# Turning the raw input rows and applying the norm's root to the products: one edit to a hybrid mixer and MoE layer

## What is computed

```
h = rmsnorm(x, norm1_g)                 # x * rsqrt(mean(x*x) + eps) * g
u = h @ w_in                            # 2048 x 5632: a (3x512), q, k, v (1024 each), c (2x512)
y_a = bg * conv3(cg * xv)               # short convolution mixer
y_b = attention(q, k, v)                # 8 heads of 128, causal, with ALiBi
y_c = silu(layernorm(conv31(a * sigmoid(gate)) + b))
x = x + concat(y_a, y_b, y_c) @ w_out
x = x + moe(rmsnorm(x, norm2_g))        # 4 groups x 8 experts, top 2 within a group
out = rmsnorm(x, final_g)
```

## Time and profile before

| | |
|---|---|
| median of three runs | 1317.46 us |
| the profiled execution: span from first to last instruction | 1315.5 us |
| time around that span (median minus span) | 2.0 us |
| instructions | 15712 |
| TensorE products busy | 1236.0 us (94%) |
| VectorE, ScalarE, GpSimd busy | 557.6, 287.5, 6.0 us |
| HBM read and written | 469.13 and 2.10 MB |

### The profile page before, as it was taken

One profiled execution on the slowest core, in us unless ns is written; L12 is line 12 of the kernel. 1 busy time (PEld: TensorE's weight loads), 2 busy tenths in 40 slices (PEclk: granted clock), 3 DMA queues, 4 the chain that ended last, 5 costly groups with the idle time before them and its releaser, 6 DMA issues.

```text
span 1315.5 us, 15712 instructions
## 1 busy us (share of the span) xinstructions
PE 1236.0 (94%) x5942; PEld 647.9 (49%) x5942; DVE 557.6 (42%) x988; ACT 287.5 (22%) x404; POOL 6.0 (0%) x27
## 2 busy tenths in 40 slices
PE   8999999999999999999898989999988999999996
PEld 7888888888874333333333333333333333333332
DVE  6575988774565323232322223223222232232234
ACT  6443454474441011101001000010010000101003
POOL 1000000000000000000000000000000000000000
PEclk9999999999999999999999999999999999999998
DMA  8655454457489999999999999999999999999996
GB/s 306 218 192 182 139 192 166 156 182 298 158 340 345 432 430 430 430 430 431 431 433 431 431 430 431 431 430 431 431 433 431 431 430 431 431 430 431 429 427 265
DMA packets 66129, 471.76 MB, mean 359 GB/s; under 512 B 6151, under 2 KB 6663, under 8 KB 39596
## 3 DMA queue, kind: packets, MB, share of 16 engines
q1 hardware_dynamic: 66092, 471.24, 87.2%
HBM read 469.13 MB, written 2.10 MB: 358 GB/s over the span
## 4 chain that ended last, share of the span: by engine, by line
PE 63%; DMA 31%; DVE 2%; issue 2%; ACT 1%; SPq 0%; DVEq 0%; ACTq 0%
DMA ring<-in_w_up 23%; PE bank L1929 21%; PE bank L1681 10%; PE bank L1689 8%; DMA zone_u<-in_w_up 8%; PE bank L1965 8%; PE bank L1978 5%; PE bank L1690 4%; PE bank L1899 1%; PE bank L1930 1%; DVE zone_u L1089 1%; PE bank L1692 1%; PE bank L2122 1%; DMA x_tok<-in_x 1%; ACT gatesT L885 1%
## 5 line engine op out<-in xcount | busy, mean ns | idle before, releaser
L1929 PE MATMUL bank<-ring,win 128*64 128x512 f32 x816 | 377.3, 617 | 41.4 <-DMA ring<-in_w_up 29.3
L1930 PE MATMUL bank<-ring,win 128*64 128x512 f32 x832 | 380.2, 610 | 0.0
L1929 PEld LDWEIGHTS bank<-ring,win 128*64 128x64 f32 x816 | 112.0, 141 | 284.3 <-issue 265.8
L1689 PE MATMUL bank<-h_both,w_hi 128*128 128x512 f32 x540 | 192.3, 398 | 1.0 <-DVE h_both L1011 0.8
L1461 DVE SCALAR_TENSOR_TENSOR x_tok<-bank,gate_of,x_tok 128x512 f32<-128x512 f32 x248 | 169.1, 744 | 30.3 <-PE bank L1978 29.3
L1965 PE MATMUL bank<-ring,hiddenT 128*64 128x512 f32 x672 | 150.8, 594 | 11.3 <-ACT gatesT L885 11.3
L413 DVE TENSOR_TENSOR w_lo<-stage,w_hi 128x2048 fp32r<-128x2048 f32 x58 | 132.4, 2288 | 64.0 <-ACT w_hi L407 63.9
L1690 PE MATMUL bank<-h_both,w_lo 128*128 128x256 f32 x540 | 151.3, 280 | 0.0
L407 ACT ACTIVATE w_hi<-stage 128x2048 fp32r<-128x2048 f32 x58 | 111.3, 1920 | 121.4 <-PE bank L1690 77.9
L877 ACT ACTIVATE rows_now<-bank,root_row 64x512 f32<-64x512 f32 x31 | 21.1, 681 | 533.1 <-PE bank L1930 533.1
L1978 PE MATMUL bank<-y_rows,gatesT 64*128 64x512 f32 x496 | 123.5, 615 | 0.0
(11 more groups left out here) (274 smaller groups left out, 1055.5 us busy)
## 6 DMA issues: line engine op xcount, KB each, us to landing
ring<-in_w_up SPq DMA_DIRECT2D x49, 2048.0 KB, 31.6
ring<-in_w_gate SPq DMA_DIRECT2D x47, 2048.0 KB, 34.8
ring<-in_w_down SPq DMA_DIRECT2D x41, 2048.0 KB, 31.6
stage<-in_w_in SPq DMA_DIRECT2D x43, 1024.0 KB, 5.0
zone_u<-in_w_down SPq DMA_DIRECT2D x19, 2048.0 KB, 31.7
zone_u<-in_w_up SPq DMA_DIRECT2D x9, 2048.0 KB, 33.6
zone_u<-in_w_gate SPq DMA_DIRECT2D x9, 2048.0 KB, 35.0
stage<-in_w_out SPq DMA_DIRECT2D x16, 1024.0 KB, 5.0
```

Source lines behind the costliest of these rows:

```text
L1689: M.matmul(dst[:, :], hi[:, at], both, start=(c == 0), stop=False)
L1929: M.matmul(dst[0:W_ROWS, :], rows_of[:, c, 0:W_ROWS], gate[:, at], start=(c == 0), stop=(c == C - 1))
L1930: ins = M.matmul(dst[UPPER, :], rows_of[:, c, 0:W_ROWS], up[:, at], start=(c == 0), stop=(c == C - 1))
```

## The change

The rows of x are turned as they are. The root (one number per token) is applied to the results. For transposed results it lies along the free axis, so the roots are spread over all partitions: VectorE multiplies the identity by each token's root (`root_diag`), TensorE multiplies that by ones, VectorE copies the result (`root_all`). GpSimd multiplies a, gate, the short convolution's output, q and k by it, cg by its square (cg and xv are multiplied with each other, so cg carries both), 128x256 each. v takes its root as the scale of its copy. x comes in column quarters, each ahead of a chunk of w_in. Row c*128+p of w_in is now channel c, partition p (before p*16+c), and g1 is loaded as 16 rows and turned by TensorE. The diff, cut:

```diff
-KEEP_START, KEEP_ROOT, KEEP_SPLIT = 48, 8, 6
+KEEP_START, KEEP_TURN, KEEP_SPLIT = 6, 8, 8
-        MASK_CONSTS, START_CONSTS, ROUTE_CONSTS = 4, 6, 9
+        START_CONSTS, MASK_CONSTS, ROUTE_CONSTS = 4, 6, 9
-        w_in = a["w_in"][0].rearrange("(p c) n -> p c n", c=C)
+        w_in = a["w_in"][0].rearrange("(c p) n -> p c n", p=P)
# SyncE
+            load_x(0)
+            for c in range(2):
+                sp.dma_start(stage[0][:, c * NB:(c + 1) * NB], chunks[0][:, c, :]).then_inc(w_early[c], 16)
+            sp.dma_start(stage[0][:, 2 * NB:]...chunks[0][:, 2:, :]).then_inc(w_loaded[0], 16)
+            for m in range(1, STAGES):
+                load_x(m)
+                sp.dma_start(stage[m]..., chunks[m]).then_inc(w_loaded[m], 16)
# GpSimd: before, ones_b, before_b and from_b are made ahead of bias_d; and after the paddings:
+            pool.wait_ge(roots_copied, 1)
+            pool.tensor_tensor(root_sq, root_all, root_all, ALU.mult).then_inc(roots_squared, 1)
+            def scaled(ready, count, at, by):
+                pool.wait_ge(ready, count)
+                pool.tensor_tensor(at, at, by, ALU.mult).then_inc(row_scaled, 1)
+            for j in range(J):
+                scaled(proj_sum, j + 1, hcT[:, j, TAPS_C - 1:HCW], root_all)
+            for j in range(J):
+                scaled(proj_sum, J + j + 1, tmpT[:, j, :], root_all)
+            for j in range(J):
+                scaled(proj_sum, 2 * J + j + 1, zT[:, j, TAPS_A - 1:ZC], root_sq)
+            for j in range(J):
+                scaled(short_tap, (TAPS_A - 1) * J + j + 1, tmpT[:, j, :], root_all)
+            for f in range(N_HALVES):
+                for n, rows_of in enumerate((qT, kT)):
+                    for j in range(J):
+                        scaled(proj_sum, (N_FIRST + 2 * f + n) * J + j + 1, rows_of[:, j, :], root_all)
# ScalarE (VectorE's order of turned_lo and w_lo is the same)
+            act.dma_start(g1_rows, a["norm1_g"][0].rearrange("(c p) -> c p", p=P)).then_inc(g1_loaded, 16)
-            (four squares and two roots ahead of everything)
+            for c in range(2):
+                turned_hi(range(c, c + 1))
+                act.wait_ge(w_early[c], 16)
+                first_chunk_hi(c)
+            turned_hi(range(2, CM))
             (w_hi[0], second half)
             for h in range(2):
+                turned_hi(range(CM + 2 * h, CM + 2 - h + 2 * h))
                 (w_hi[1], half h)
-                turned_hi(range(2 + h, 3 + h))
+            turned_hi(range(2 * CM - 1, 2 * CM + 2))
             split_hi(act, 0, 0, 2)
-            turned_hi(range(4, C // 2))
+            turned_hi(range(2 * CM + 2, 3 * CM))
+            (Square of x's tile 0, 2048 wide; VectorE squares tile 1)
+            turned_hi(range(3 * CM, 3 * CM + 2))
             split_hi(act, 0, 0, 3)
+            turned_hi(range(3 * CM + 2, C))
+            (root of both tiles)
-                    act.wait_ge(proj_sum, J + j + 1)
+                    act.wait_ge(row_scaled, J + j + 1)          # ahead of each sigmoid
# VectorE, after split_lo(dve, 0, 0, 3) and turned_lo(14, 15): mean, reciprocal, two root_diag, then
             V.tensor_copy(parT...)
+            dve.wait_ge(roots_spread, 1)
+            V.tensor_copy(root_all, bank[6][:, 0:S]).then_inc(roots_copied, 1)
# TensorE
+            def turn(cs):
+                for c in cs:
+                    pe.wait_ge(x_loaded[c // CM], 16)
+                    if c >= CM:
+                        pe.wait_ge(turned_dve, c - CM + 1)
+                    for t in range(T):
+                        ins = M.transpose(turned_in(c)[:, t * P:(t + 1) * P], x_tok[:, t, c * P:(c + 1) * P], ident[:, :])
+                    ins.then_inc(turned, 1)
             for m in range(STAGES):
-                if m == STAGES - 1:
-                    turn_params()
                 for i in range(CM):
+                    if c == C - 2:
+                        turn_params()
+                    if c == C - 1:
+                        spread_roots()
                     (the eight products of channel c)
+                    if m < STAGES - 1:
+                        turn(range(c + CM, c + CM + 1))
             for b in range(1, N_FIRST):
                 if b == 1:
+                    pe.wait_ge(roots_copied, 1)
+                        pe.wait_ge(row_scaled, SCALED_Q + (2 * f + 1) * J + h + 1)   # ahead of head h's scores
```

More of the change, by code:

```diff
@@ L207, in turned_in @@
         def turned_in(c):
-            at, half = (4 + c % 4, c // 4) if c < 2 * CM else (4 + c // 2 % 4, c % 2)
-            return bank[at][:, half * S:(half + 1) * S]
+            half = c // CM % 2
+            return bank[4 + c % CM][:, half * S:(half + 1) * S]
         def x_rows(t, b):
@@ L390, in slot_of, with load @@
             return piece_at(e, k)[0]
[L392 to L396, removed]
+        def load(sp, b, chunks):
+            for m, src in enumerate(chunks):
+                sp.wait_ge(lo_made, chunk(4 * b + (m - 4)))
                 dst = stage[m][:, :]
@@ L436, in _, with load_x @@
         def _(sp):
[L437 to L441, removed]
-            chunks = columns(w_in, FIRST_BLOCKS[0])
-            for c in range(0, CM, 2):
-                sp.dma_start(stage[0][:, c * NB:(c + 2) * NB].rearrange("p (c n) -> p c n", c=2),
-                             chunks[0][:, c:c + 2, :]).then_inc(w_loaded[0] if c else w_early, 16)
+            x_in = a["x"][0].rearrange("(t p) n -> p t n", p=P)
+            def load_x(q):
+                at = slice(q * NB, (q + 1) * NB)
+                sp.dma_start(x_tok[:, :, at], x_in[:, :, at]).then_inc(x_loaded[q], 16)
+            chunks = columns(w_in, FIRST_BLOCKS[0])
+            load_x(0)
+            for c in range(2):
+                sp.dma_start(stage[0][:, c * NB:(c + 1) * NB], chunks[0][:, c, :]).then_inc(w_early[c], 16)
+            sp.dma_start(stage[0][:, 2 * NB:].rearrange("p (c n) -> p c n", c=2), chunks[0][:, 2:, :]).then_inc(w_loaded[0], 16)
+            for m in range(1, STAGES):
+                load_x(m)
+                sp.dma_start(stage[m][:, :].rearrange("p (c n) -> p c n", c=CM), chunks[m]).then_inc(w_loaded[m], 16)
             for n, c0 in enumerate(FIRST_BLOCKS):
-                load(sp, n, columns(w_in, c0), 0 if n else 1)
-                if n == 0:
+                if n:
+                    load(sp, n, columns(w_in, c0))
+                else:
                     for row, src in ((R_WA, a["conv_a_w"][0]), (R_WC, a["conv_c_w"][0]), (R_CB, a["conv_c_b"]),
@@ L656, in _ @@
             pool.wait_ge(rw_ready, RW_STEPS)
-            pool.wait_ge(turned, C // 2)
+            pool.wait_ge(turned, C)
             pool.wait_ge(par_turned, 1)
@@ L675, in _ @@
             act.wait_ge(warm_set, 2)
[L676 to L683, removed]
             def first_chunk_hi(c):
@@ L989, in _ @@
             dve.sem_inc(att_copied, HALF_HEADS)
[L992 to L1000, removed]
             def first_chunk_lo(c):
@@ L1009, in turned_lo @@
                 for c in cs:
-                    dve.wait_ge(turned_act, c + 1 if c < 2 * CM else 2 * (c // 2) + 2)
+                    dve.wait_ge(turned_act, c + 1)
                     V.scalar_tensor_tensor(hT_lo[:, c, :], turned_in(c), g1[:, c:c + 1],
                                            hT_hi[:, c, :].bitcast(F32), ALU.mult, ALU.subtract).then_inc(turned_dve, 1)
[L1014 to L1029, removed]
+            dve.wait_ge(g1_turned, 1)
+            V.tensor_copy(g1[:, :], bank[0][:, 0:C]).then_inc(g1_made, 1)
+            dve.wait_ge(g1_made, 1)
+            for c in range(2):
+                turned_lo(range(c, c + 1))
+                first_chunk_lo(c)
+            turned_lo(range(2, CM))
             dve.wait_ge(hi_made, 1)
@@ L1642, in keep, with spread_roots @@
                 for i in range(n):
-                    M.matmul(bank[0][:, 0:P], ones_b[:, :], before_b[:, :], start=True, stop=True)
[L1645 to L1649, removed]
-                    for c in (2 * k, 2 * k + 1):
-                        ins = M.transpose(turned_in(c)[:, t * P:(t + 1) * P], h_tok_c[:, t, c, :], ident[:, :])
-                    if t == T - 1:
-                        ins.then_inc(turned, 1)
+                    M.matmul(bank[1][:, 0:P], ones_b[:, :], before_b[:, :], start=True, stop=True)
+            def turn(cs):
+                for c in cs:
+                    pe.wait_ge(x_loaded[c // CM], 16)
+                    if c >= CM:
+                        pe.wait_ge(turned_dve, c - CM + 1)
+                    for t in range(T):
+                        ins = M.transpose(turned_in(c)[:, t * P:(t + 1) * P], x_tok[:, t, c * P:(c + 1) * P], ident[:, :])
+                    ins.then_inc(turned, 1)
+            def spread_roots():
+                pe.wait_ge(diag_made, T)
+                pe.wait_ge(turned_dve, C)
+                for t in range(T):
```

(11 more changed lines are left out.)

103 lines of the change are left out of this document (56 added, 47 removed).

## The result

| | before | after |
|---|---|---|
| median of the runs | 1317.63 us (11 runs, 1317.33 to 1319.80) | 1321.25 us (11 runs, 1320.44 to 1321.79) |
| ratio | | 1.0024 (95%: 1.0015 to 1.0032) |
| span of the profiled execution | 1315.5 us | 1319.5 us |
| first product | 13.57 us | 8.32 us |
| first product of block 1 | 38.97 us | 40.03 us |

The changed kernel is slower: the medians lie 3.6 us apart (0.27%), the ratio of all the runs gives 0.24%, just above the 0.2% (2.6 us) that a measurement tells from no change and with an interval that does not reach 1. The median is 3.1 us above the forecast of 1318.1 and 0.2 above the upper end of the range, 1321.0. Measured by the ratio, from the 1317.46 that the forecast started at, it is 1317.46 x 1.0024 = 1320.6, which is inside. It came out at the upper edge.

The account below looks back on a forecast made before the run. TensorE was taken to bound the mixers until 390 us, the DMA the experts after. Span 1315.5 plus 0.6 for block 1's later start, plus about 2.0 around it, gave 1318.1 us; range 1314.5 to 1321.0.

Parts of the forecast that it names:

- the first rival: Key block: GpSimd's q multiplies and VectorE's taps block each other, adding 1.5 us, 1319.6 in all; chance 0.28.
- Part 1: Kernel start: squares, means, roots and scaling leave the chain; first product at 7.5 us, a lead of 6.1.
- Part 2: TensorE's clock at the start: rises at 10 us, so products from 7.5 run at half speed, 1.25 us lost.
- Part 3: Block 0, supply of the first six channels: channel 5 ends at 18.6 us, range 17.5 to 19.8.
- The rival of a clock that stays low: Block 0: TensorE stays at 1.2 GHz far in; a rise at 15 us gives 1320.6; chance 0.15.
- Part 4: Block 0: three new waits from instruction order, 1.6, 1.6 and 1.4 us; block 1 begins at 39.6, +0.6 us.
- the 5.09 of the sum: Block 0: time from channel 5's end through turn, copy, w_hi and w_lo to channel 8's start, 5.09 us.
- Part 5: SyncE's load queue: 0.4 us more issue, passed on to parameter, router and block 1 loads; costs nothing.
- Part 6: GpSimd's 33 multiplies, 0.6 us each: covered at gate and scores; q's beside the taps taken as 0 of 0 to 2.4.
- The sign that the forecast had named: Key block: w_lo of chunk 2, at 161.29 before, keeps its old distance from block 1.
- v's root rides on its copy: At v in the heads: the root is applied within the existing copy, counted as covered, with no added time.

Follow-up runs that it names:

- the runs with one edit each: Changed kernel with the splits of chunks 2 and 3 one turned channel forward: 1318.09 us; or with block 1's first w_lo ahead of the roots' copy: 1319.29 us.
- the last run: Changed kernel with splits of chunks 2 and 3 one turned channel forward, block 1's first w_lo before the roots' copy, q's multiplies held back: 1314.80 us.
- the run with multiplies: Kernel before plus four GpSimd 128x256 multiplies of two SBUF inputs into unused memory, released by q's sums in the first half: 1319.67 us.

## Where the forecast was right, and where it was off

The point was 1318.1 and the measurement 1321.25; in the profiled executions 1316.1 was forecast and 1319.5 came. By the router 3.66 us of lateness had built up against 0.6 forecast. The mechanism of block 0 was forecast rightly; in the key block it was the first rival's mechanism that held, not the forecast's. By the steps:

- **Part 1, off by 0.8 us.** 7.5 (7.2 to 8.0) for the first product; it came at 8.32. The step that failed is "the first quarter of x is 512 KB, as the first load of before, whose square starts at 4.88": it landed at 5.69, and TensorE's turns start at 5.74 behind a wait for it:

```profile
0.79 4.90 DMA x_tok<-in_x
```

Same bytes, but stretches of 512 columns (2 KB) from two token tiles instead of 1024 columns (4 KB) from one, with g1's load beside it and other loads behind it. Which of these made it later is open; a load of the same columns in another cut was not run. The eight turns then took 1.76 us from start to start (5.74 to 7.50), not 1.41, since they ran before the clock rose; the forecast's rounding from 7.2 to 7.5 happened to cover that.
- **Part 2, off the other way.** The clock rose at about 9.4, not 10, and cost 18.59 - 8.32 - 9.8 = 0.5 us instead of 1.25. The two misses met: channel 5 ended at 18.59, against 18.6 in Part 3, so this number came out right by luck. The rival of a clock that stays low did not happen.
- **Part 4, right in the waits, 0.4 us short in the sum.** Three waits were forecast at channel 8, channel 12 and block 1, of 1.6, 1.6 and 1.4 us; they are 1.45, 1.45 and 1.42, and the runs with one edit each show that the first two hang on one order and the third on another. From channel 5's end to block 1 the sum gave 21.0; it took 21.44. Left out was the restart: in the chain, the first product after each of the first two waits has 0.50 us instead of 0.23, 0.54 together, and channel 14, behind the parameters' turn, lost 0.2 in the same way. The two ways from the end of the turn to w_lo were 0.17 shorter each than the 5.09 of the sum, which hid part of it. So block 1 began at 40.03, 0.4 above 39.6 and inside its 38.5 to 40.8.
- **Part 5, right.** No wait of TensorE, VectorE or ScalarE for the loads that were passed shows in the changed kernel's first 60 us.
- **Part 6, the step that made the error.** "I take 0 from it" for the q multiplies beside the taps: it was 1.38 us on the taps (4.62 against 3.24), 1.47 at the end of the key block, almost exactly the 1.5 of the first rival with its mechanism, its place and its price. The row chosen as nearest, the router's multiply beside VectorE instructions with a PSUM input, was far in just the property that counts; the text said so and still took its value. That the other multiplies are covered held: no wait at the gate or the scores. The sign that the forecast had named, the key block's w_lo of 161.29 at its old distance from block 1, failed too: it runs at 164.15, 124.12 us after block 1's start instead of 122.32. A second term was put at nothing without a reason: v's root rides on its copy, and that copy is slower for it, 1.27 us for two against 1.09. TensorE's wait for ScalarE behind it grew from 0.34 to 0.52 us in each half of the heads, 0.18 us twice. The Trainium skill (ScalarE: Activation LUTs, What ACT_TABLE_LOAD costs) puts a per-partition pointer operand at about 93 ns each; these two copies agree with it.
- **The sum of it.** 0.43 from the later start of block 1, 0.42 in block 1 (the restart after its wait and a slower pace), 1.47 in the key block, twice 0.18 behind v's copy, and 0.34 of pace before the second q block's copy make the 3.0 us between the 0.6 forecast and the 3.66 found.

No measurable change was given 0.68 and slower 0.20; the result lies just on the slower side of the bound. The chances: a lock at q (0.28) was the likeliest rival and what happened, on top of the forecast's block 0. By itself it gives 1319.6, within the bound of no change. It took the small terms left out besides, 1.5 us in sum and all on one side, to pass it. Most of them were omissions of one kind: a sum made of durations in steady state has no restart and no second pace in it.

## What to carry to other kernels

Where a change gives the critical engine a head start, ask what the helpers' instruction order makes of it: here 4.3 us of a lead of 5.25 went into three waits for splits that stood behind work that they did not need, and three small moves turned a slower kernel into one 3.3 us faster than the kernel before. GpSimd's multiplies on SBUF inputs were free only where the VectorE work beside them, itself with two SBUF inputs, had no deadline next: in the last run they cost VectorE more (5.20 us for eight taps) and the kernel nothing. When the nearest row differs from the case in the very property that a rule names, it is no evidence for zero; take a value between the ends (here 0 and 2.4 us, of which 1.47 came).

## What the runs showed of the hardware beyond that

**A wait of TensorE costs more than its length.** In the chain, which counts from end to end, the first product of 512 columns after each wait for w_lo has 0.47 to 0.51 us instead of 0.23, even after a wait of 0.26 us (the key block in the run without q multiplies: 0.51). By starts two parts of it can be seen. In the stream a product starts 0.17 us before the recorded end of the one before it (24.55 for 0.28, the next at 24.66), and that overlap is lost once. And the second product of 512 columns starts 0.45 us after the first (23.51, 23.96) instead of 0.35. Together they make some 0.25 us on top of the wait.

**Two paces of one and the same block.** Between the copies ahead of block 1 and behind it lie 22.22 us in the six of the ten kernels in which block 1 begins without a wait, and 24.21 in the four in which it begins with one of 1.42. Restart and wait explain 1.66 of the 1.99; the other 0.33 is pace: each of the first channels of block 1 takes 1.38 or 1.39 us in the kernel before, the last four 1.41, and all but the first take 1.41 or 1.42 in the changed one. So a wait at the start of block 1 went with a slower block each time. The other place does not fit that: from v's first copy to the second q block's, with the faster copies of the kernel before, it is 26.82 us there and 27.16 in the run with multiplies, and with the slower copies 27.00 or 27.34, and no new wait lies in it. Two such places cost the changed kernel 0.7 us. What sets the pace stays open: no run varied it alone.

**Which of the two engines is held up differs from run to run.** The same move of q's multiplies was made in two kernels. In both the first multiply starts just behind the first tap (168.72 after 168.54; 164.31 after 164.14). With the move alone the eight taps keep 3.28 us and GpSimd's first multiply takes 8.09; with all three edits the taps take 5.20 us and GpSimd's four multiplies 3.56 together. The second half of the heads repeats it: taps 3.28 and four multiplies 10.01 in the one, 5.19 and 3.55 in the other. What decides it stays open; each is one trace.

**GpSimd's multiplies stretch.** Four of 128x256 take 2.83 us beside VectorE's sums out of PSUM (at 178.99 in the changed kernel), 0.7 each, and this is what they become beside the splits and the gate:

```profile
37.77 2.59 POOL L673 TENSOR_TENSOR y_rows<-y_rows 128x256 f32<-128x256 f32 x1 [2.21 <-DVE y_rows L1074]
...
114.57 10.26 POOL L677 TENSOR_TENSOR zone_u<-zone_u,y_rows 128x256 f32<-128x256 f32 x4 [25.03 <-DVE zone_u L1146]
```

One takes 2.59 us beside a w_lo of 2.29, four take 10.26. A cover computed with 0.6 us for one, as in Part 6, is several times too thin; it held here, with no wait of TensorE at the gate, because the slack was larger still.
